# Scores of a differential attention as plain fp32 products in two row groups, in place of three products of high and low parts

## The reference

```python
def diff_attention(q, k, v, lam):
    scale = 1.0 / math.sqrt(DK_A)                 # DK_A = 64
    def attend(qb):
        s = jnp.einsum('bqhcd,bshcd->bhcqs', qb, k).astype(jnp.float32) * scale
        p = jax.nn.softmax(s, axis=-1)
        p = p[:, :, 0] - lam[None, :, None, None] * p[:, :, 1]
        return jnp.einsum('bhqs,bshe->bqhe', p.astype(v.dtype), v)
    return sweep_query_blocks(attend, q)          # blocks of 128 queries
```

## Time and profile before

| | us |
|---|---|
| median of 3 runs | 1294.17 (1294.02 to 1296.85) |
| the profiled execution | 1295.62 |
| its span | 1293.8 |
| TensorE matmul busy | 1236.3 |
| TensorE weight load busy | 993.7 |
| VectorE busy | 759.3 |
| ScalarE busy | 602.1 |
| GpSimd busy | 252.8 |
| mean granted TensorE clock | 0.987 |

### The profile page before, as it was taken

The page is one execution under the profiler, slowest core; times in us unless marked ns, Lnnn a source line. Parts: engine busy times, 40 slices in busy tenths (PEclk is TensorE's granted clock), DMA queues, the critical chain, the costliest instruction groups (busy, mean ns, idle before and its releaser), DMA issues.

```text
span 1293.8 us, 17785 instructions
## 1 busy us (share of the span) xinstructions
PE 1236.3 (96%) x6751; PEld 993.7 (77%) x6751; DVE 759.3 (59%) x1167; ACT 602.1 (47%) x1259; POOL 252.8 (20%) x426
## 2 busy tenths in 40 slices
PE   4699988999999999999999999999999999999994
PEld 3355867888888888878787888888787878887883
DVE  4334686748667486554545455464646564769593
ACT  5223314554645546464555555455555655312223
POOL 2010311203021030122212122122223322210102
PEclk9899998999999999999999999999999999999997
DMA  9998452112112121222222221212124423646455
GB/s 338 386 380 284 121 179 65 50 49 86 50 49 75 45 94 50 78 70 72 65 60 78 65 85 53 80 58 80 58 70 136 137 72 107 239 120 244 153 181 179
DMA packets 131093, 156.51 MB, mean 121 GB/s; under 512 B 8144, under 2 KB 98416, under 8 KB 130240
## 3 DMA queue, kind: packets, MB, share of 16 engines
q1 hardware_dynamic: 118032, 111.22, 26.5%
q0 software_dynamic: 12976, 44.15, 10.6%
HBM read 144.18 MB, written 11.16 MB: 120 GB/s over the span
## 4 chain that ended last, share of the span: by engine, by line
PE 86%; DMA 5%; DVE 3%; ACT 2%; POOL 1%; issue 1%; SPq 1%; ACTq 0%; DVEq 0%; POOLq 0%
PE z_ps L607 23%; PE z_ps L609 22%; PE z_ps L608 22%; PE ring L696 5%; PE ring L731 3%; PE ring L796 3%; DMA gate_raw<-in_w_ada_dram 2%; PE ring L800 2%; PE ring L629 1%; DMA ada_raw<-in_w_ada_dram 1%; DVE gate_acc L1455 1%; PE ring L609 1%; PE ring L608 1%; PE ring L803 1%; PE ring L607 1%
## 5 line engine op out<-in xcount | busy, mean ns | idle before, releaser
L607 PE MATMUL z_ps<-w_hi,xt_hi 128*128 128x512 f32 x1360 | 563.9, 415 | 7.5 <-DVE xt_lo L1226 3.2
L609 PE MATMUL z_ps<-w_hi,xt_lo 128*128 128x512 f32 x1360 | 532.8, 392 | 0.0
L608 PE MATMUL z_ps<-w_lo,xt_hi 128*128 128x512 f32 x1360 | 531.6, 391 | 0.0
L883 ACT ACTIVATE w_hi<-w_raw 128x512 fp32r<-128x512 f32 x272 | 170.4, 628 | 373.8 <-PE z_ps L609 332.1
L1232 DVE TENSOR_TENSOR w_lo<-w_raw,w_hi 128x512 fp32r<-128x512 f32 x272 | 194.6, 718 | 203.7 <-ACT w_hi L883 203.3
L607 PEld LDWEIGHTS z_ps<-w_hi,xt_hi 128*128 128x128 f32 x1360 | 256.3, 188 | 68.4 <-issue 17.4
L609 PEld LDWEIGHTS z_ps<-w_hi,xt_lo 128*128 128x128 f32 x1360 | 255.8, 188 | 56.7
L608 PEld LDWEIGHTS z_ps<-w_lo,xt_hi 128*128 128x128 f32 x1360 | 257.3, 189 | 39.4
L1309 DVE TENSOR_REDUCE small<-s_sb 128x2 f32<-128x1536 f32 (+1 forms) x60 | 88.3, 1472 | 23.6 <-ACT s_sb L883 22.3
L1000 ACT ACTIVATE s_sb<-s_sb,small 128x768 f32<-128x768 f32 (+1 forms) x120 | 97.9, 820 | 1.6 <-DVE small L1309 1.6
L1627 POOL TENSOR_TENSOR sg<-sg,zs 128x128 f32<-128x128 f32 (+1 forms) x60 | 37.9, 632 | 282.6 <-DVE sg L1292 282.1
(11 more groups left out here) (161 smaller groups left out, 1341.8 us busy)
## 6 DMA issues: line engine op xcount, KB each, us to landing
w_raw<-in_w_in_dram SPq DMA_DIRECT2D x192, 256.0 KB, 3.1
ada_raw<-in_w_ada_dram SPq DMA_DIRECT2D x64, 512.0 KB, 11.0
w_raw<-in_w_out_dram SPq DMA_DIRECT2D x64, 256.0 KB, 3.5
gate_raw<-in_w_ada_dram POOLq DMA_DIRECT2D x12, 1024.0 KB, 7.2
o_spill<-row_st POOLq DMA_DIRECT2D x14, 320.0 KB, 4.1
row_st<-o_spill POOLq DMA_DIRECT2D x14, 320.0 KB, 3.8
x_sb<-in_x_sample_dram SPq DMA_DIRECT2D x4, 1024.0 KB, 10.1
w_raw<-in_w_in_dram POOLq DMA_DIRECT2D x16, 256.0 KB, 6.4
```

The source lines that it names most:

```text
L607: pe.matmul(out, hi_l, hi_r, start=start, stop=False)
L608: pe.matmul(out, hi_l, lo_r, start=False, stop=False)
L609: return pe.matmul(out, lo_l, hi_r, start=False, stop=stop)
L883: return act.activation(out, in_, ACT.Copy, **kw)
```

## The change

Queries and keys of mixer A are stored as they are, in two new fp32 tiles `q_f` and `k_f` that lie where the high and low parts of mixer B's queries and keys were. `qk_his` copies into them and now frees the bank itself; `qk_los` has nothing to do for mixer A. `s_pair` makes one plain fp32 matmul where it made three: two for the prompt tile, four for a latent tile, in the order component 0's 512 keys, component 1's tail, component 1's 512 keys, component 0's tail.

```diff
+    q_f, e = place("q_f", [P, TILES * P], F32, r1)
+    k_f, _ = place("k_f", [P, NKEY + P], F32, e + 4 * TILES * P)
...
             if g == "D":
-                return [(n, 0, S, q_hi[0][:, 0:S], q_lo[0][:, 0:S], True),
-                        (n + 1, 0, S, k_hi[0][:, 0:S], k_lo[0][:, 0:S], True),
-                        (n + 2, 0, C + P, k_hi[0][:, S:S + C + P], k_lo[0][:, S:S + C + P], False),
-                        (n + 2, C + P, P, q_hi[0][:, S:S + P], q_lo[0][:, S:S + P], True)]
+                return [(n, 0, S, q_f[:, 0:S], None, True),
+                        (n + 1, 0, S, k_f[:, 0:S], None, True),
+                        (n + 2, 0, C + P, k_f[:, S:S + C + P], None, False),
+                        (n + 2, C + P, P, q_f[:, S:S + P], None, True)]
...
-                terms = ((q_hi, k_hi), (q_hi, k_lo), (q_lo, k_hi))
-
-                def product(out, c_, i, k0, kn, turn=None):
-                    of_q, of_k = terms[i]
-                    ins = pe.matmul(out, of_q[0][rows[c_], q0:q0 + P], of_k[0][rows[c_], k0:k0 + kn],
-                                    start=(i == 0), stop=(i == 2))
-                    if turn is not None and i == 2:
-                        filled(ins, turn)
-                    return ins
+                def product(out, c_, k0, kn):
+                    return pe.matmul(out, q_f[rows[c_], q0:q0 + P], k_f[rows[c_], k0:k0 + kn], start=True, stop=True)
 
                 if t == 0:
-                    outs = [claim(n + c_)[:, 0:P] for c_ in range(2)]
-                    for i in range(3):
-                        for c_ in range(2):
-                            product(outs[c_], c_, i, NKEY, P, n + c_)
+                    for c_ in range(2):
+                        filled(product(claim(n + c_)[:, 0:P], c_, NKEY, P), n + c_)
                     return
-                main = [claim(n)[:, 0:512], claim(n + 1)[:, 0:512]]
+                main = [claim(n + c_)[:, 0:512] for c_ in range(2)]
                 rest = claim(n + 2)
-                tail = [rest[:, 256 * c_:256 * (c_ + 1)] for c_ in range(2)]
-                for c_, of_tail, i in ((0, 0, 0), (1, 1, 0), (1, 1, 1), (0, 0, 1), (1, 1, 2), (1, 0, 0), (0, 0, 2), (1, 0, 1),
-                                       (0, 1, 0), (0, 1, 1), (1, 0, 2), (0, 1, 2)):
-                    if of_tail:
-                        if c_ == 0 and i == 0:
-                            pe.wait_ge(tail_done, tails)
-                        ins = product(tail[c_], c_, i, 512, NKEY - 512, n + 2 if c_ == 0 else None)
-                        if c_ == 1 and i == 2:
-                            ins.then_inc(tail_done, 1)
-                    else:
-                        product(main[c_], c_, i, 0, 512, n + c_)
+                filled(product(main[0], 0, 0, 512), n)
+                product(rest[:, 256:512], 1, 512, NKEY - 512).then_inc(tail_done, 1)
+                filled(product(main[1], 1, 0, 512), n + 1)
+                pe.wait_ge(tail_done, tails)
+                filled(product(rest[:, 0:256], 0, 512, NKEY - 512), n + 2)
...
             def qk_his(a):
-                for n, col, w, hi, _, _ in qk_parts(a):
+                for n, col, w, hi, lo, last in qk_parts(a):
                     wait_full(act, n)
-                    copy(hi, RB(n)[:, col:col + w]).then_inc(qk_hi_done, 1)
+                    ins = copy(hi, RB(n)[:, col:col + w])
+                    if lo is not None:
+                        ins.then_inc(qk_hi_done, 1)
+                    elif last:
+                        ins.then_inc(free_sem(n), 1)
...
             def qk_los(a):
+                if group_kind(a) == "D":
+                    return
```

## The result

The changed kernel takes 1311.45 us (median of 4 runs, 1311.28 to 1312.98) against 1295.23 us (4 runs): ratio 1.0129, 95% interval 1.0116 to 1.0142, or +16 us. (The ratios in this text are formed from all runs, so they differ slightly from those of two medians.) The profiled executions took 1311.34 and 1295.62 us, +15.7, and their spans stand as far apart. The direction was forecast, the size was four times the forecast, and the time lies outside the range.

What follows compares the result with a forecast made beforehand. TensorE's own stream was taken to bound the kernel. Latent score blocks 32 x 0.15 = +4.8 us and prompt blocks 8 x -0.07 = -0.6 gave +4.2 us on a median of 1294.17: 1298.4 us, range 1296 to 1304.

Steps and rivals of the forecast that it cites:

- What bounds the kernel: In mixer A's stage TensorE's own stream sets the length: one head 72.11 us long, TensorE busy for 72.11 us.
- VectorE's relief: In mixer A's stage 32 subtractions, 17.8 us, leave VectorE; counted as worth nothing in kernel time.
- Price of plain fp32: In mixer A's score blocks a record passes its columns twice, a product four times; 0.109 us per 128 columns of a record.
- The sum of +4.2 us: Mixer A's score blocks: 32 x 0.15 = +4.8 us for latent tiles, 8 x -0.07 = -0.6 for prompt tiles.
- Overlap of the row groups in plain fp32: In mixer A's score blocks both row groups run together as now, latent block 1.50 us; chance 0.78.
- the cover of the wait for the tail: Before a latent block's last product: tail out at 0.7 us, first row group busy until 0.97, so the wait is hidden.
- A wait for the tail ahead of the last product: Sign in a latent tile's score block that would show the cover of the wait for the tail wrong.
- The rival with program order: In score blocks no record starts before those ahead in the program: latent block 1.93 us, sum +18.9 us, 1313; chance 0.09.
- The waits that could be given back: TensorE's waits of 1.0, 0.3 and 0.2 us in mixer A's stage go: +2.7 us, 1296.9; chance 0.05.

Runs made afterwards that it cites:

- the last experiment: The changed kernel, but VectorE still makes the 32 subtractions of queries and keys (into unused memory) and frees the banks; 1311.41 us.
- same experiment: The kernel before, with the third product of component 1's tail placed behind component 0's third 512-column product; 1303.88 us, ratio 1.0067.

## Why the prediction was wrong

- **What bounds the kernel** was right: the stage grew by 14.6 us, its score blocks by 15.4, and VectorE's relief gave nothing back, as the last experiment shows.
- **Price of plain fp32** was right. A record passes its columns twice, 512 columns take 0.43 to 0.44 us, and with the wait covered the block is 1.49 us (forecast 1.50), the prompt tile's 0.42 (0.41). The sum of +4.2 us is what the order with the tail first measures: 1299.36 - 1295.46 = +3.9, and +4.0 over the blocks of its trace.
- **Overlap of the row groups in plain fp32** was right; both start together, and no row shows it lost.
- **The failed step is the cover of the wait for the tail**, which I put at the tail's own end, 0.7 us into the block, against 0.97 until which the row group is busy anyway. The end is told only after that of the 512-column product ahead of it in the program, at about 1.12, and the load follows at 1.22, its matmul streams from 1.33. That is 0.36 us after 0.97 in each of 32 blocks, 11.5 us, and 4.2 + 11.5 = 15.7. The order with the tail first took these 11.5 us out of the blocks again, and three lengths of the product ahead moved the load accordingly. A wait for the tail ahead of the last product was the sign that the prediction itself had named for an error in this step, and it appeared. I had even read the 0.1 us that the wait costs in the kernel before, and took it for a fixed cost where it was the visible end of something that grows with the products; "without that cover it would cost the 0.1 us that it costs now" was wrong as well.
- **The rival with program order** named 1313 us, next to the measured time, by a mechanism that did not happen: the block is 1.85 and not 1.93 us, and starts do pass each other. The Trainium skill ("TensorE: Matmul & The Clock Gate", section The mechanism) says that matmuls are in program order at start and at end. Of this the runs bear out the end as it is told to the semaphore (raised at 1.18 us behind the 512-column product, at 0.71 with the tail first), and not the start (644.46 before 644.68). I weighed the rule against rows that show starts only, found them against it, and dropped the half that no row had spoken of.
- **The waits that could be given back** were rightly counted as nothing: the one of 1.0 us on the last output rows and that of 0.2 us are in the changed kernel too. The one of 0.3 us is gone, but it is gone as well with the subtractions kept and in the high and low kernels with another order, so VectorE's relief isn't what removed it.

What stays open: the semaphore is raised 0.01 to 0.06 us after the later of the two ends, the tail's own and that of the product ahead. The ends in these records are modelled, so this may be the model's error or a time of its own. How the chip keeps the telling in order isn't shown either, only that it does between two row groups. The profiled execution with 256 columns ahead of the tail has a span 2.6 us shorter than the one with the tail first, but the stage of mixer A takes 539.89 us in both; the difference lies ahead of it and behind it, in an execution whose mean granted clock was 0.990 against 0.987.

## What to carry to other kernels

Where products of two row groups run side by side and one waits for the other's result, put the awaited product first in the program, not only first in its row group: in these runs its end was told only after that of the product ahead of it. When products are merged into fewer and longer ones, price each wait anew with the length of the product ahead of the awaited one. And a rule that has two halves needs a row for each before it is set aside.

## What the runs showed of the hardware

- Matmuls of different row groups start out of program order (644.46 before 644.68 with the tail's third product later), yet their ends reach a semaphore in program order: for a tail finished at 0.70 us the semaphore was raised at 0.71, 0.73, 0.94 and 1.18 us with none, 256, 384 and 512 columns of plain fp32 ahead of it, and the waiting load came 0.04 us later each time.
- A wait in TensorE's queue also holds products of the other row group that stand behind it: one that could have started at about 0.93 us started at 1.06 (same experiment).
- Plain fp32 products of 64 rows overlap across two row groups: eight records, 3072 column passes for each group or 1.28 us at 2.4 GHz, in a block of 1.49 us.
